# S5 branch of a two-block transformer kernel: chunked states, a table for the tokens inside a chunk, and a new order of steps

## The chip, the cores and the metric

One core of one Trainium2 chip (trn2) runs the whole program. The metric is device microseconds of that core for one execution; smaller is better. Three executions of the kernel before were timed, and one more was taken by the profiler.

## The reference, cut to what matters

Two transformer blocks run one after the other on x of 512 tokens by 1024 channels. The second block has three inputs that meet: an S5 state space branch, a sparse attention branch (called dsa) and two gates. The change touches the S5 branch alone:

```
def s5_branch(xs, a_re, a_im, log_dt, b_re, b_im, c_re, c_im, d_skip, w_glu, b_glu):
    xg = xs.reshape(bsz, seq, 32, 16)          # 32 groups of 16 channels, 64 complex states each
    lb = exp((a_re + i a_im) * dt)             # decay and turn of each state
    bb = (lb - 1) / a * b                      # input matrix
    bu = einsum('blgc,gpc->blgp', xg, bb)
    s[t] = lb * s[t-1] + bu[t]                 # scan over 512 tokens
    y = real(einsum('blgp,gcp->blgc', s, c)) + d_skip * xs
    y = gelu(y)
    val, gate = split(y @ w_glu + b_glu)
    return val * sigmoid(gate)
```

The 2048 complex states are 16 sets of 128 (one set is two groups). Since the decay has a magnitude and an angle, the kernel turns bu back by the angle times t, scans real and imaginary parts with the magnitude alone, and turns the result forward again.

## The kernel before, in words

**Weight stream.** All large matrix products go through 1976 blocks of 128x128 weights, each against 512 tokens. A block is three TensorE instructions (lines 723, 724, 726: high half times high half, low half of the weight, low half of the data). Eight blocks are a unit. A unit is loaded by SP's queue into one of four raw buffers (L2342), rounded to its high half by ScalarE (L1126) into one of four buffers, negated (L1135), and GpSimd's queue adds the rest by an accumulating DMA (L2212). Five units are done by VectorE instead (L2146). Each engine's program walks the same list of blocks with a fixed lead (class Units), so a wait on any one engine ahead of its share of a unit delays all later units.

**First block.** Lines 827 to 861 for TensorE: input products, the recurrent branch, pooling, `w_out`, then 22 pairs of `w_up` tiles (22 times 16 blocks, the loop at L860; called the up stage below) and 8 `w_down` tiles of 22 blocks. ScalarE in this loop does, for each j, the tap of tile j (L1292), the gelu of tile j-1 (L1297), which needs VectorE's two taps of tile j-1 (L1883, L1886), and the tap of tile 22+j. Each is preceded by its share of the weight stream.

**S5 constants.** VectorE makes them in the up and down stages: powers of the angle (L1766), cosines and sines of the first 32 tokens (L1785), then for each of 16 sets a table of cosines and sines of 512 tokens, built by doubling (L1798 to L1816, 18 instructions a set). SP stores each table in memory (`store_table`, L2383) and GpSimd's queue loads it back three sets ahead of use (`load_table`, L2240). The input matrix is formed once (`s5_matrices`, L1915), turned by eight 128x128 transposes on TensorE (`turn_b`, L865), split in high and low halves and spread by 12 DMAs into `wst` (L2436).

**Mixed stage.** After `w_down` and a norm, the first four tiles of `w_in_2` give xs (four tiles of 128 channels). Then five generators on each engine are stepped by one string, ORDER: `d` the attention branch (56 steps), `s` S5 (64), `g` the 16 gate tiles in 64 steps of two blocks, `u` the glu in 32 steps of two blocks, `a` the attention projection in 16 steps of two blocks. The string fixes the order of the instructions on all five engines at once. On TensorE an S5 set takes two matmuls (L925, 96 rows: xs high, low, high against B high, high, low); VectorE turns them (four products, L1987 to L1993), GpSimd adds pairs (L2264, L2266), VectorE scans 512 tokens twice (L1997, L1999) and turns forward (L2002 to L2006); after four sets TensorE sums 16 matmuls of 32 columns over 512 tokens (L914). The high and low halves of xs are stacked in partitions by DMAs from one place of the core's memory to another (L2452; the first two by ScalarE's queue, L1335).

Results in PSUM use eight banks in turn. SBUF slots of 2 KB a partition are given out by `layout`, and a slot's next user waits for the last one.

```
def block(tile, kk, pair, out, start, stop):
    ...
    matmul(out, wh, sr(pair, kk, "hi"), start=start, stop=False)
    matmul(out, wl, sr(pair, kk, "hi"), start=False, stop=False)
    ...
    mm = matmul(out, wh, sr(pair, kk, "lo"), start=False, stop=stop)
```

Of the kernel before, what the change touches and what calls it, by code (L numbers as in the profile page):

```python
# [37 lines left out]
for _n, _c in VECS:  # L38
# [6 lines left out]
         ("lim", 16), ("den", 16), ("ta", 16), ("tb", 16), ("cre", 16), ("cim", 16),   # L45
         ("mod", 48), ("gs1", 8), ("gs2", 8), ("r1", 4), ("r2", 4), ("r", 28), ("wi", 16), ("m8", 8),
         ("need", 1), ("nm", 16), ("rsm", 16)]
# [5 lines left out]
assert _o <= 900  # L53
# [17 lines left out]
UP_STEPS = tuple(int(j > 1 and j % 2 == 0) for j in range(22))  # L71


# [3 lines left out]
def mod_home(u):  # L77
# [6 lines left out]
    "dsssggsdsgdsgsssssggsggsggsdgggsggsssggssggsggsgsgsgssdsssggggssgssgsgsdsgsggdgsgggssgsggg"  # L84
    "ssssggggsgggsdgssssgssgdsssggsgdssggssdgsgdgsdsgdsdudududdudduudugdggduddududuuddduuuuuuud"
    "uududdudgdududdudddduududdddddduaudddduaaaaauaaaaaaaaaa"
)

ROOTS = [1, 2, 3, "ki", "ck", 5, 6]

# [109 lines left out]
class Kit:  # L200


    def __init__(self, nc, top, x_d, w_d, mod_d, cond_d, vec_d, cst_d, inv_d, ssm_d, uk_d, spill_d,
                 tab_d, xs_d, out_d):
# [3 lines left out]
        self.cond_d, self.xs_d = cond_d, xs_d  # L208
# [27 lines left out]
        self.wst_in = sig("wst_in", 16)  # L236
        self.st_in = [sig(f"st_in{i}", 16) for i in range(8)]
        self.tab_out = [sig(f"tab_out{i}", 16) for i in range(2)]
        self.tab_in = [sig(f"tab_in{i}", 16) for i in range(3)]
# [13 lines left out]
        self.sml = sb("sml", [128, 900])  # L253
# [26 lines left out]
    def place_rows(self, part, c):  # L280

        return self.sr("bt", part).rearrange("p (j c n) -> p c j n", c=2, j=4)[:, c]
# [16 lines left out]
def layout(k):  # L299
# [125 lines left out]
    run([("ssm_b",)], 2, top=True)  # L425
    run([("ssm_c",)], 3, top=True)
    run([("uk",)], 2, top=True)
    run([("tabw",)], 4, top=True)

    def constants():  # L430
        for _ in range(8):
            yield
        run([("trig",)], 2)
        take("tq")
        yield
        for _ in range(16):
            yield
        for n in ("tabw", "tq", "trig"):
            give(n)

    consts = constants()
    for _ in range(8):
        next(consts)
# [7 lines left out]
    for j in range(22):  # L451
        take("up", j)
        if j:
            glu_1(j - 1)
        take("up", 22 + j)
        for _ in range(UP_STEPS[j]):
            next(consts, None)
        if j == 11:
            for i in range(NMB):
                give("mb", i)  # L460
            give("cond", 0)
# [5 lines left out]
    for m in range(8):  # L467
        squares("g", m)
        squares(3, m)
        next(consts, None)  # L470
        if m == 4:
            for n in (0, 1):
                take("sq5", n)
            for n in (0, 1):
                give("sq5", n)
        if m == 5:
            for h in ("hi", "lo"):
                run([("bt", h)], 2)
            give("ssm_b")
    for j in range(22):  # L480
        give_pair("act1", j)
    run([("wst", j) for j in range(4)], 8)
    for h in ("hi", "lo"):
        give("bt", h)
# [5 lines left out]
    run([("tbuf",)], 6)  # L490
# [3 lines left out]
    def stacks(s):  # L494
        if s == 0:
            pair("xq", 0)
        for q in (s, s + 1):
            take("st", q)
        if s % 4 == 2:
            give_pair("xq", s // 4)  # L500
            if s < 14:
                pair("xq", s // 4 + 1)

    def s5():
        def outputs(s):
            if s % 4 == 3:
                for q in range(s - 3, s + 1):
                    for n in ("q1", "q2", "q3", "q4"):
                        give(n, q)
                pair("ys", s // 4)  # L510
                give("xs", s // 4)
                give("wst", s // 4)

        stacks(0)
        for s in range(16):
            if s % 2 and s < 15:
                stacks(s + 1)
            give("st", s)
            take("q1", s)
            take("q2", s)  # L520
            yield
            take("q3", s)
            take("q4", s)
            yield
            yield
            if s:
                outputs(s - 1)
                yield
        outputs(15)
        yield  # L530
        give("ssm_c")
        give("tbuf")
        for i in range(7, NMC):
            run([("mc", i)], 2, top=True)
# [157 lines left out]
def tensor_engine(k, T):  # L692
# [166 lines left out]
    done.release(*[("v2", i, h) for i in range(8) for h in ("hi", "lo")])  # L859
    for j in range(22):  # L860
# [4 lines left out]
    def turn_b(c):  # L865

        b = take("s5_turn", c)
        T.wait_ge(at("s5_b"))
        for j in range(4):
            mm = transpose(b[:, 128 * j:128 * j + 128],  # L870
                           k.ssm_b[:, c, 4 * j:4 * j + 4, :].rearrange("p s n -> p (s n)"),
                           k.ident)
        mm.then_inc(*done.tick(("s5_turn", c)))
        give("s5_turn", c)

    for m in range(8):
        tile("w_down", m, range(22), "act1", [3, "g"] if m == 7 else ())
        if m == 5:
            turn_b(0)
            turn_b(1)  # L880
            done.release(("ssm_b",))
# [20 lines left out]
    def s5():  # L902
        def outputs(last):

            j, i = divmod(last, 4)
# [1767 lines left out]
```

## Time and profile before

| what | value |
|---|---|
| median of 3 runs | 1562.13 us (1561.71 to 1562.28) |
| the profiled execution: its span, first to last instruction | 1561.0 us |
| its own time | not given apart from the span; the span lies 1.1 us under the median |
| TensorE matmul busy | 1512.8 us, 97% |
| TensorE weight load busy | 1193.3 us, 76% |
| VectorE busy | 842.4 us, 54% |
| ScalarE busy | 842.2 us, 54% |
| GpSimd busy | 276.5 us, 18% |
| mean granted clock of TensorE | 0.990 |
| moved by DMA | 329.37 MB, 211 GB/s |
| chain that ended last | TensorE 76%, VectorE 14%, ScalarE 5% |

Busy time is a union over one engine's instructions. Matmuls overlap in the pipeline, so the cost of one in a row of its like is the distance from its start to the next start, not its own duration: a block of three costs 0.70 us (three starts 0.23 us apart), while each instruction is shown as about 0.4 us long. A plain fp32 matmul is shown as two records; a transpose is one. The granted clock is a share of full speed, 2.4 GHz; the lower level is 1.2 GHz, shown as 0.5 in a stretch that lies wholly at it.

### The profile page before, as it was taken

How to read it: one execution, taken by the hardware profiler on the slowest of the kernel's cores; microseconds unless marked ns; L12 is line 12 of the kernel's file. 1: busy time of each engine (PE TensorE's matmuls, PEld its weight loads, DVE VectorE, ACT ScalarE, POOL GpSimd, SP SyncE). 2: the span in 40 equal slices, each digit the busy share in tenths (PEclk: the TensorE clock that was granted, in tenths of full speed). 3: DMA queues.
4: the chain of work that ended last, by engine and by line, in shares of the span. 5: the costliest groups of instructions: out<-in, count | busy, mean ns of one | idle time of the engine just before them, and what ended most of it. 6: DMA issues, size and time to landing. Idle time of an engine off the chain costs nothing.

```text
span 1561.0 us, 17900 instructions
## 1 busy us (share of the span) xinstructions
PE 1512.8 (97%) x6688; PEld 1193.3 (76%) x6688; DVE 842.4 (54%) x1640; ACT 842.2 (54%) x1080; POOL 276.5 (18%) x307
## 2 busy tenths in 40 slices
PE   9999999999999999999999897899999999999998
PEld 7877888888878888888877575576777888888886
DVE  6788634555596766545448899975663122110011
ACT  5777877845565555544455353567436444444441
POOL 1111111111111111111114442121011111111111
PEclk9999999999999999999999999999999999999999
DMA  9777787799999988999899894494478998888882
GB/s 266 176 184 170 177 194 184 182 311 299 273 263 265 220 207 210 230 273 241 215 229 291 232 248 130 126 279 167 136 197 201 233 231 182 195 180 194 189 180 81
DMA packets 99221, 329.37 MB, mean 211 GB/s; under 512 B 11568, under 2 KB 13104, under 8 KB 99008
## 3 DMA queue, kind: packets, MB, share of 16 engines
q0 software_dynamic: 36704, 133.56, 45.5%
q1 hardware_dynamic: 58608, 187.33, 35.7%
q10 hardware_dynamic: 3824, 7.34, 1.3%
q8 instruction: 53, 0.87, 0.2%
q14 instruction: 32, 0.26, 0.0%
HBM read 179.69 MB, written 18.87 MB: 127 GB/s over the span
## 4 chain that ended last, share of the span: by engine, by line
PE 76%; DVE 14%; ACT 5%; issue 2%; DMA 2%; POOL 1%; SPq 0%; ACTq 0%; DVEq 0%
PE ps L723 24%; PE ps L726 24%; PE ps L724 24%; DVE pl_f L2052 2%; DVE sml L2049 2%; DVE pl_f L1829 1%; ACT whi L1126 1%; DVE pl_f L1999 1%; DVE pl_r L1546 1%; ACT wlo L1135 1%; POOL pl_f L2264 1%; DMA pl_r<-pl_r 1%; PE ps L767 1%; DMA wlo<-raw 1%; PE ps L914 1%
## 5 line engine op out<-in xcount | busy, mean ns | idle before, releaser
L723 PE MATMUL ps<-pl_r,whi 128*128 128x512 f32 x1976 | 788.9, 399 | 10.0 <-DVE pl_f L1633 3.2
L724 PE MATMUL ps<-pl_r,wlo 128*128 128x512 f32 x1976 | 784.2, 397 | 0.0
L726 PE MATMUL ps<-pl_r,whi 128*128 128x512 f32 x1976 | 784.1, 397 | 0.0
L723 PEld LDWEIGHTS ps<-pl_r,whi 128*128 128x128 f32 x1976 | 373.5, 189 | 108.6 <-issue 13.4
L726 PEld LDWEIGHTS ps<-pl_r,whi 128*128 128x128 f32 x1976 | 373.3, 189 | 91.4 <-DVE pl_r L1563 0.9
L724 PEld LDWEIGHTS ps<-pl_r,wlo 128*128 128x128 f32 x1976 | 373.4, 189 | 89.0 <-issue 0.5
L2212 POOL DMA_DIRECT2D wlo<-raw x238 | 204.0, 859 | 1092.8 <-ACT wlo L1135 1068.2
L1126 ACT ACTIVATE whi<-raw 128x1024 fp32r<-128x1024 f32 x247 | 259.7, 1052 | 185.4 <-PE ps L726 140.1
L1135 ACT ACTIVATE wlo<-raw 128x1024 fp32r<-128x1024 f32 x238 | 248.6, 1045 | 0.0
L1546 DVE TENSOR_TENSOR pl_r<-pl_f,pl_r 128x512 fp32r<-128x512 f32 x120 | 84.5, 704 | 49.3 <-ACT pl_r L1155 32.9
L2184 DVE TENSOR_TENSOR pl_f<-ps,pl_f 128x512 f32<-128x512 f32 x22 | 15.2, 691 | 177.6 <-PE ps L726 177.6
L1292 ACT ACTIVATE pl_f<-ps,vec 128x512 f32<-128x512 f32 x44 | 34.0, 777 | 101.1 <-PE ps L726 101.1
L1155 ACT ACTIVATE pl_r<-pl_f 128x512 fp32r<-128x512 f32 x42 | 26.3, 631 | 106.4 <-DVE pl_f L2184 79.9
L2161 DVE SCALAR_TENSOR_TENSOR pl_f<-ps,sml,pl_f 128x512 f32<-128x512 f32 x16 | 12.0, 750 | 119.8 <-PE ps L726 119.8
L1145 ACT ACTIVATE pl_f<-pl_f 128x512 f32<-128x512 f32 x38 | 23.8, 629 | 73.5 <-DVE pl_f L2161 51.1
L1883 DVE SCALAR_TENSOR_TENSOR pl_f<-ps,vec,pl_f 128x511 f32<-128x511 f32 x44 | 32.9, 748 | 54.1 <-ACT pl_f L1292 54.1
L1829 DVE CUSTOM_DVE_ANT_0 pl_f<-pl_f,pl_f 128x1024 f32<-128x1024 f32 x48 | 58.0, 1219 | 0.1
L1935 DVE TENSOR_TENSOR pl_f<-pl_f,ps 128x512 f32<-128x512 f32 x8 | 5.5, 689 | 62.7 <-PE ps L726 62.7
L1499 ACT ACTIVATE pl_f<-ps 128x512 f32<-128x512 f32 x22 | 13.1, 597 | 45.1 <-PE ps L726 44.9
L1886 DVE SCALAR_TENSOR_TENSOR pl_f<-ps,vec,pl_f 128x511 f32<-128x511 f32 x44 | 33.0, 750 | 1.6
L1646 DVE SCALAR_TENSOR_TENSOR pl_f<-pl_f,pl_f 128x512 f32<-128x512 f32 x20 | 12.9, 689 | 36.2 <-ACT pl_f L1232 36.2
L1633 DVE SCALAR_TENSOR_TENSOR pl_f<-ps,vec,pl_f 128x511 f32<-128x511 f32 (+1 forms) x30 | 22.4, 748 | 17.8 <-ACT pl_f L1213 17.0
(234 smaller groups left out, 1188.3 us busy)
## 6 DMA issues: line engine op xcount, KB each, us to landing
raw<-in_w SPq DMA_DIRECT2D x245, 512.0 KB, 5.3
wlo<-raw POOLq DMA_DIRECT2D x238, 512.0 KB, 6.2
pl_f<-in_mod SPq DMA_DIRECT2D x48, 512.0 KB, 7.3
tab<-pl_f SPq DMA_DIRECT2D x16, 512.0 KB, 6.3
pl_f<-tab POOLq DMA_DIRECT2D x16, 512.0 KB, 7.5
xs<-pl_f SPq DMA_DIRECT2D x16, 256.0 KB, 8.8
pl_f<-xs SPq DMA_DIRECT2D x16, 256.0 KB, 5.1
spill<-pl_f ACTq DMA_DIRECT2D x16, 256.0 KB, 4.8
```

What stands on the lines that cost most here:

```text
L723: matmul(out, wh, sr(pair, kk, "hi"), start=start, stop=False)
L724: matmul(out, wl, sr(pair, kk, "hi"), start=False, stop=False)
L726: mm = matmul(out, wh, sr(pair, kk, "lo"), start=False, stop=stop)
L1126: act(k.whi[:, u % NHI, :], k.raw[:, u % NRAW, :], ACT.Copy).then_inc(*k.w_hi.tick(("w_hi", u)))
L1135: act(k.wlo[:, u % NLO, :], k.raw[:, u % NRAW, :], ACT.Copy, scale=-1.0).then_inc(*k.w_neg.tick(("w_neg", u)))
L1292: act(sb("up", j), ps("w_up", j), ACT.Identity, bias=vc("conv_f_b", j), scale=vc("conv_f_w", 44 + j)).then_inc(*done.tick(("up_tap", j)))
L1546: tt(sr(pair, m, "lo"), src, sr(pair, m, "hi").bitcast(F32), ALU.subtract).then_inc(*done.tick((pair, m, "lo"), *freed_by))
L1829: V.eng.tensor_tensor_reduce(r, r, sb(*c), 1.0, 0.0, ALU.mult, ALU.add, sm("mod", u)).then_inc(*done.tick(("mod_used", u), *([mod_home(u)] ...
L1883: stt(f[:, 1:S], b[:, 0:S - 1], vc("conv_f_w", j), f[:, 1:S], ALU.mult, ALU.add).then_inc(*done.tick())
L1886: stt(f[:, 0:S - 1], b[:, 1:S], vc("conv_f_w", 88 + j), f[:, 0:S - 1], ALU.mult, ALU.add).then_inc(*done.tick(("up", j), ("w_up", j)))
L2049: V.eng.max(m8, cur).then_inc(*done.tick())
L2212: P.eng.dma_start(k.wlo[:, u % NLO, :].bitcast(F32), k.raw[:, u % NRAW, :], accum_op=ALU.add).then_inc(*k.w_lo[u % NLO].tick(("w_lo", u)))
```

## The change

The 16 sets become four groups q of four sets i. A chunk is four tokens (TAPS = 4), so there are 128 chunks (NCH).

- ScalarE writes xs(q) with the four tokens of a chunk apart; SP stores it in memory (`stack_out`) and loads it back (`stack`) with 32 channels times 4 tokens on the partitions and, for each set, 128 chunks along them. This replaces the rounding of xs into halves and the DMAs that stacked them.
- Input: B times the powers 3, 2, 1, 0 of lb (`inputs`, VectorE, 6 instructions of 512 elements a group), turned by 8 transposes a group (`turn_b`), 32 in all instead of 8. For a group TensorE then does 8 plain fp32 matmuls of 128 tokens (chunks) instead of 8 of 512.
- VectorE turns, scans and turns forward 4 sets at once: 4 + 4 products of 512 elements and 8 scans of 128 a group.
- Output: C times the powers 0 to 4 (`outputs`, 6 instructions of 640), and `taps` on TensorE, 32 small matmuls a group: the table of what a token in a chunk adds to itself and to the later ones. The output sums 16 matmuls of 128 from that table and 32 of 127 from the states, all of 32 columns.
- `turning`: cosines and sines of 128 chunks, 14 VectorE instructions a group, instead of 16 tables of 512.
- Constants are made at fixed tiles of the up and down stages (CONSTS for VectorE, TURNS for TensorE and ScalarE), stored by SP one tile later (`stores`), and loaded back as four tables a group, 1.75 MB (`load_tables`), on SP's queue instead of GpSimd's.
- ORDER has 16 steps of S5 instead of 64, done in the order of PLACES, and the other letters stand in a new order among each other.

```
+TAPS = 4
+PLACES = [("b", 0), ("t", 0), ("b", 1), ("c", 0), ("b", 2), ("t", 1), ("c", 1), ("o", 0),
+          ("t", 2), ("b", 3), ("c", 2), ("t", 3), ("c", 3), ("o", 1), ("o", 2), ("o", 3)]
+CONSTS = {2: ("p", 0), 4: ("b", 0), 6: ("c", 0), 8: ("t", 0), 10: ("b", 1), 12: ("c", 1), 14: ("t", 1),
+          16: ("b", 2), 18: ("c", 2), 20: ("t", 2), 22: ("b", 3), 23: ("c", 3), 24: ("t", 3)}
+TURNS = {6: ("b", 0), 8: ("c", 0), 12: ("b", 1), 14: ("c", 1), 18: ("b", 2), 20: ("c", 2),
+         23: ("b", 3), 26: ("c", 3)}
+ORDER = (
+    "dsggsssggggdsggsgsdgssgggddgggsssdsggggdgsgdgsgggsgdggggsgdguuugggduugddggddddgggggddgdgud"
+    "ddugdgggggggdggggddggdgududduuggdudugdudduduuuduuuuudduudududdudduudduddddugaddddduaaauaaaaa"
+    "aaaaaaa"
+)
 # TensorE, up and down stages
+    def taps(q):
+        T.wait_ge(at("s5_c", q), at("s5_b", q))
+        for i in range(4):
+            for c in range(2):
+                for r in range(TAPS):
+                    mm = matmul(b[rows, 128 * i + 32 * r:128 * i + 128]...,
+                        sb("sbp")[:, 512 * c + 128 * i + 3:512 * c + 128 * i + 128:TAPS],
+                        cp[:, c, 0:TAPS - r, i], start=c == 0, stop=c == 1,
+                        tile_position=(0, 32 * r))
     for j in range(22):
         tile("w_up", j, range(8), "h2")
         tile("w_up", 22 + j, range(8), "h2")
+        turns(j)
 # TensorE, S5
-        for s in range(16):
-                matmul(b, k.wst[0:96, j, i, c, :], sr("st", s)[0:96], start=True, stop=True)
+            if step == "b":
+                for c in range(2):
+                    T.wait_ge(at("bt", q), at("st", q))
+                    for i in range(4):
+                        mm = matmul(b[:, cols], sb("bt", q)[...], sb("st", q)[:, cols], ...)
+            elif step == "o":
+                for n in range(TAPS):
+                    for i in range(4):
+                        matmul(y[32 * i:32 * i + 32, NCH * n:NCH * n + NCH], sb("tt", q)[...],
+                               sb("st", q)[:, 128 * i:128 * i + 128], ..., tile_position=(0, 32 * i))
+                for c, state in ((0, "q1"), (1, "q3")):
+                    for n in range(TAPS):
+                        for i in range(4):
+                            mm = matmul(y[32 * i:32 * i + 32, NCH * n + 1:NCH * n + NCH], ...,
+                                sb(state, q)[:, 128 * i:128 * i + 127], ...)
 # VectorE, constants
+    def outputs(q):
+        V.wait_ge(done.now(), at("ssm"), at("bt_out", q), *freed("scp"))
+        if q:
+            V.wait_ge(at("s5_taps", q - 1), at("cp_out", q - 1))
+        tt(re, cre, lr, ALU.mult).then_inc(*done.tick())
...
 # SP
     for j in range(22):
         if j > 1:
             weights(16)
+        if j:
+            stores(j - 1)
...
+    load_tables(0, "bt", "cs", "tt", "cp")
     weights(32)
+    def stack_out(q):
+        Q.wait_ge(at("xs", q))
+        dma(k.stk_d[q], sb("xs", q)).then_inc(*k.st_out[q].tick(("xs_out", q)))
+    def stack(q):
+        Q.wait_ge(at("xs_out", q), *freed("st", q))
+        dma(sb("st", q).rearrange("p (i n) -> p i n", i=4),
+            k.stk_d[q].rearrange("(i c) (j n) -> (c j) i n", i=4, j=TAPS)).then_inc(
+            *k.st_in[q].tick(("st", q)))
+    for q in range(4):
+        stack_out(q)
+    stack(0)
+    load_tables(1, "bt", "cs", "tt", "cp")
     def s5():
+        for step, q in PLACES:
+            if step == "b" and q < 3:
+                stack(q + 1)
+            if step == "t" and q in (0, 1):
+                load_tables(q + 2, "bt", "cs", "tt", "cp")
+            yield
```

All four tables of a group share one semaphore, so each is counted as there when the last of the four has landed. `outputs(q)` uses the buffer from which the turned B of the same group is stored (`bt_out`), for its products in between.

## Rows read from the trace of the kernel before

**Rows 1.** The page's part 2: busy tenths in 40 slices of 39 us

```profile
PE   9999999999999999999999897899999999999998
DVE  6788634555596766545448899975663122110011
PEclk9999999999999999999999999999999999999999
DMA  9777787799999988999899894494478998888882
```

**Rows 2.** Windows: up stage and mixed stage; stretch length, busy by engine, clock, DMA

```profile
405.00:750.00 345.00, 344.84 (x1491) 278.07 (x1490) 220.67 (x525) 179.08 (x215) 52.20 (x62) 1.00 0.94 238
819.26:1100.32 281.06, 253.55 (x1229) 181.53 (x1227) 228.87 (x439) 152.38 (x249) 87.44 (x83) 0.96 0.74 207
```

**Rows 3.** Waits of TensorE between 815 and 1115 us: total us, times, longest

```profile
PE ps L809 <- DVE sml L1541: 6.2, 1, 6.2
PE ps L965 <- DVE pl_f L2130: 5.3, 1, 5.3
PE ps L914 <- DVE pl_f L2006: 4.4, 1, 4.4
PE ps L925 <- DMA pl_r<-pl_r: 3.5, 1, 3.5
...
PE ps L981 <- DVE pl_f L2060: 1.5, 1, 1.5
PE ps L987 <- ACT pl_f L1368: 1.4, 1, 1.4
PE ps L925 <- DVE pl_f L1975: 1.1, 1, 1.1
```

**Rows 4.** Timeline of TensorE: start us, us of the merged run, line, count

```profile
931.48 0.63 PE L925 MATMUL ps<-pl_r,pl_r 96*128 96x512 f32 x2
932.04 3.64 PE L914 MATMUL ps<-pl_f,pl_f 128*32 128x512 f32 x32
935.61 0.50 PE L723 MATMUL ps<-pl_r,whi 128*128 128x512 f32 x1
...
1094.82 2.38 PE L1020 MATMUL ps<-cst,pl_f 128*128 128x128 f32 x20
1097.14 1.09 PE L1031 MATMUL ps<-cst,sml 128*64 128x128 f32 x16
1098.07 2.32 PE L1040 MATMUL ps<-pl_f,pl_f 128*64 128x512 f32 x16
```

**Rows 5.** Groups of VectorE between 815 and 1115 us, forms apart

```profile
L1997 DVE TENSOR_TENSOR_SCAN pl_f<-ps,pl_f 128x512 f32<-128x512 f32 x16 | 19.6, 1223 | 2.9 <-POOL pl_f L2264 2.8
...
L1987 DVE TENSOR_TENSOR pl_f<-ps,pl_f 128x512 f32<-128x512 f32 x16 | 10.9, 683 | 9.0 <-PE ps L925 9.0
...
L2074 DVE TENSOR_TENSOR_SCAN pl_f<-pl_f 128x384 f32<-128x384 f32 x1 | 1.0, 960 | 0.0
...
L2074 DVE TENSOR_TENSOR_SCAN pl_f<-pl_f 128x256 f32<-128x256 f32 x1 | 0.7, 692 | 0.0
```

**Rows 6.** The page's part 6: DMA issues, KB each, median us to landing

```profile
wlo<-raw POOLq DMA_DIRECT2D x238, 512.0 KB, 6.2
...
tab<-pl_f SPq DMA_DIRECT2D x16, 512.0 KB, 6.3
...
xs<-pl_f SPq DMA_DIRECT2D x16, 256.0 KB, 8.8
pl_f<-xs SPq DMA_DIRECT2D x16, 256.0 KB, 5.1
```

**Rows 7.** Timeline of ScalarE and GpSimd around the end of one `w_up` tile

```profile
573.03 0.78 ACT L1292 ACTIVATE pl_f<-ps,vec 128x512 f32<-128x512 f32 x1 [2.41 <-PE ps L726]
573.71 1.05 ACT L1126 ACTIVATE whi<-raw 128x1024 fp32r<-128x1024 f32 x1
...
576.00 0.85 POOL L2212 DMA_DIRECT2D wlo<-raw  x1 [4.23 <-ACT wlo L1135]
```

More of the change, by code:

```diff
@@ L424, in layout @@
         give("x", m)
[L425 to L443, printed above, removed]
+    for n, w in (("ssm_b", 2), ("ssm_c", 2), ("trig", 2), ("sbp", 2), ("sbt", 2), ("scs", 2),
+                 ("scp", 3), ("stt", 1)):
+        run([(n,)], w, top=True)
     def glu_1(j):
@@ L469, in layout @@
         squares(3, m)
[L470 to L479, printed above, removed]
     for j in range(22):
         give_pair("act1", j)
-    run([("wst", j) for j in range(4)], 8)
-    for h in ("hi", "lo"):
-        give("bt", h)
+    for n in ("ssm_b", "ssm_c", "trig", "sbp", "sbt", "scs", "scp", "stt"):
+        give(n)
+    run([("uk",)], 2)
+    for q in range(4):
+        for n in TABS:
+            run([(n, q)], TABS[n][1] // S)
     give("sq", "g", 0)
@@ L489, in layout @@
         take("xs", j)
-    run([("tbuf",)], 6)
+    for q in range(4):
+        take("st", q)
     for m in range(8):
         give("xw", m)
[L494 to L502, printed above, removed]
-    def s5():
[L505 to L514, printed above, removed]
-        for s in range(16):
[L516 to L520, printed above, removed]
-            yield
[L522 to L532, printed above, removed]
+    def s5():
+        for step, q in PLACES:
+            if step == "t":
+                for n in ("q1", "q2", "q3", "q4"):
+                    take(n, q)
+            elif step == "c":
+                give("bt", q)
+            elif step == "o":
+                for n in ("q2", "q4", "q1", "q3"):
+                    give(n, q)
+                for n in ("cs", "tt", "cp"):
+                    give(n, q)
+                give("st", q)
+                take("yg", q)
+                give("xs", q)
+                pair("ys", q)
+                give("yg", q)
+            yield
         for i in range(7, NMC):
@@ L919, in s5 @@
-        take("mags")
-        for s in range(16):
-            j, i = divmod(s, 4)
-            for c in range(2):
-                b = take("bu", c, s)
-                T.wait_ge(at("wst"), at("st", s))
-                matmul(b, k.wst[0:96, j, i, c, :], sr("st", s)[0:96], start=True, stop=True).then_inc(
-                    *done.tick(("bu", c, s), *([("st", s)] if c else []),
-                               *([("wst", j)] if c and i == 3 else [])))
-                give("bu", c, s)
-            yield
-            yield
-            yield
-            if s:
-                outputs(s - 1)
-                yield
@@ L1303, in scalar_engine @@
         up(22 + j)
+        turns(j)
     gelu(21)
@@ L1819, in vector_engine, with s5_constants @@
+    def s5_constants(n):
+        what, q = CONSTS.get(n, (None, 0))
+        if what == "p":
+            powers()
+        elif what == "b":
+            inputs(q)
+        elif what == "c":
+            outputs(q)
+        elif what == "t":
+            turning(q)
     steps = 0
@@ L2423, in sync_engine @@
         dma(sb("xw", m), k.xs_d[m]).then_inc(*k.x_in[m].tick(("x_back", m)))
-    Q.wait_ge(*freed("ssm_b"), *freed("ssm_c"))
-    dma(k.ssm_b, k.ssm_d[:, 0:2]).then_inc(*k.ssm_in.tick())
-    dma(k.ssm_c[:, 0:2], k.ssm_d[:, 2:4]).then_inc(*k.ssm_in.tick(("ssm",)))
+    for m in range(8):
+        weights(8)
+        stores(21 + m)
+        weights(14)
+    for u in units.ahead():
+        load(u + NRAW)
+    load_tables(0, "bt", "cs", "tt", "cp")
     Q.wait_ge(*freed("uk"))
     dma(k.uk, k.uk_d).then_inc(*k.uk_in.tick(("uk",)))
-    for m in range(8):
-        weights(22)
-        if m:
-            store_table(8 + m)
```

546 lines of the change are left out of this document (295 added, 251 removed).

## The prediction

> **What bounds the kernel now.** First the page's slices: TensorE is at 9 tenths nearly everywhere, so work taken from another engine pays only where TensorE waits for it; VectorE is full in slices 21 to 25, and there TensorE dips [rows 1]. Then two windows. In the up stage TensorE is busy 344.84 of 345 us at clock 1.00: nothing can be gained there, and each microsecond of new TensorE work costs one. In the mixed stage (281.06 us from the first S5 matmul to the end of attention) it is busy 253.55 us, so 27.5 us are idle, at a mean clock of 0.96 [rows 2]. A clock of 0.96 with 0.5 as its lower level means 8% of the stretch, 22.5 us, at half speed, in which 11 us were lost. The waste is some 38.7 us. Its waits [rows 3]: 6.2 for a reciprocal on VectorE, 5.3 and 4.4 and 1.5 and 1.1 for VectorE (a reciprocal is nothing in itself: VectorE is late, with 228.87 busy us in 281), 1.4 for ScalarE, 3.5 for the stacking DMA. These sum to 23.4; some 4 us are small waits of attention, on rows not shown, which the change does not touch.
>
> **VectorE gets light in the mixed stage.** Before: 16 sets by eight products of 0.683 us and two scans of 1.223 us [rows 5], 87.4 + 39.1 = 126.5 us. After: 4 groups by eight products, 21.9 us, and 32 scans of 128 elements. The scans of 384 and 256 take 0.960 and 0.692 [rows 5], so 128 less is 0.27 less, and one takes 0.43: 13.7 us. Gone are 91 us of 229, and 138 in a stage of 240 to 280 us no longer set the pace. S5 is then done after about 27 g steps; attention gets its VectorE time when it asks. I take the VectorE waits and ScalarE's as gone (19.9 us); what is late next is the entry.
>
> **The entry of the mixed stage.** S5's first group needs xs through memory. It is written after xs(3) at about 808 us; a store of xs takes 8.8 us to land, a load back 5.1 [rows 6]. The sum is 822 us; the new load has pieces of 512 bytes, no row shows such a one, and between no more than 5.1 and twice that I add 1.5. The order asks for it at 819.3, after step d: a wait of 4 us (0 to 12). The second group's turned B shares a semaphore with 1.75 MB of tables issued right behind that load, some 9 us at the stage's 207 GB/s [rows 2], so they land at about 826 if nothing else is under way, and TensorE asks at 826, two g (2.8 us) after its first; weights and stacks share the engines: 3 us more (0 to 8). After a wait of 3.5 to 6 us the trace shows a stretch at the lower clock: 3.5 us lost. The traffic of this entry (three groups of tables, 5.5 MB, stacks and saves, beside the weights) meets DMA engines that are 8 to 9 tenths busy already in slices 21 to 23 [rows 1]: 3 us for late weights (0 to 10). With attention's 4 us, new waste is 4 + 3 + 3.5 + 3 + 4 = 17.5 us against 38.7: **21.2 us gained**, between 33 (only attention's waits and 2 more stay) and 1.
>
> **TensorE work, outputs.** One group of 16 matmuls of 32 columns by 512 took 935.61 - 932.04 = 3.57 us [rows 4], four of them 14.3 us. After: 48 matmuls by 128 a group, 192 in all, 384 records. If four neighbours overlap as before, the tokens streamed are 12 times 128 a group against 4 times 512: 3/4 of 14.3, 10.7 us. If each record costs what the nearest shape does (64 columns by 128: 16 records in 98.07 - 97.14 = 0.93 us, 0.058 each [rows 4]), it is 22.3 us. That row is at two neighbours at once and is full with 128 tokens, so it excludes no more than it shows; I take 12, nearer the same-width row: **-2.3**. The input matmuls: two of 512 took 932.04 - 931.48 = 0.56 us here [rows 4] and 0.47 where a block follows, 7.5 in all; 32 plain ones of 128 are 64 records of 0.11 (a transpose is 2.32/20 = 0.116 with its lead-in [rows 4]), 7.0: **-0.5**.
>
> **TensorE work, constants.** 24 more transposes at 0.116: **+2.8**. Taps, 128 matmuls, 256 records: overlapped in fours, the widest of each four sets 32 times 128 tokens, two records of 0.112 (3.57/8 for 512 tokens, a quarter of it for 128): 7.1 us; at 0.058 a record 14.8; with no overlap (80 tokens on average) 18. I take 7.5, for the output row shows the overlap: **+7.5**. All of it lies in the up and down stages where TensorE is full, so all of it shows.
>
> Here the Trainium skill speaks against the change. TensorEngine Tiling (Array Packing), section Instruction Overhead, says each matmul has about 60 cycles of overhead on trn2 and warns against taking the tiling factor from a dimension that is already small. Sixty cycles at 2.4 GHz are 25 ns a record, an estimate from that page, and 640 records at 25 ns are 16 us against my 19.5: by it the sum would stay. Tensor Engine: Matmul & The Clock Gate, section Back-to-back issue gap, gives about 81 ns for each load and matmul pair of 128 tokens, and by it outputs and taps would take 52 us. Row L1031 at 58 ns already contradicts the 81; no row here is shorter than its streaming, so no run shows the 25.
>
> **VectorE, ScalarE and SP in the up stage.** VectorE's constants: 12 products of 512 and 640 a group and 14 short ones, some 14.4 us a group, 58 us, and 5 us of powers, against 16 tables of about 4.9 us and the old matrix: less than before, with VectorE at 221 of 345 us [rows 2]. Covered by TensorE's lead in eight banks. But `outputs(q)` waits for the store of the turned B. Relative to the end of the w_up pair in which the turn stands: transposes 0.9, ScalarE's two copies to 2.4, its next unit to 4.4, accumulate landed 6.2 later (the tile of the row: tap at 573.03, accumulate issued at 576.00 [rows 7], [rows 6]), and only then does SP, which waits for that unit, come to the store: about 11, landed at 17 (14 to 21). Six products of 0.83 end it at 22, two taps at 23.6. TensorE asks for its taps at 23.3 and ScalarE's gelu, which then waits 5 us, holds the conversion that TensorE needs at about 36 and gets at 33. So this stall of VectorE for 15 us, four times, is just covered: **+1** (0 to 24). If the cover goes, TensorE stops for weights, since gelu stands ahead of them on ScalarE.
>
> GpSimd loses 16 table issues and 24 of 32 additions, SP gains 16 table loads, 32 stores and 8 stack transfers for 16 stores and 60 small ones: at 0.3 to 0.6 us of issue they hide behind its waits for units. The powers and the smaller stack rounding cost nothing on the path.
>
> **Sum.** -21.2 - 2.3 - 0.5 + 2.8 + 7.5 + 1 = -12.7 us. From the span of 1561.0 that is 1548.3; the median of the runs lies 1.1 us above it, so 1549.4, told as **1549**. A measurement of this kernel can tell about 0.2%, 3.1 us, from no change.
>
> **Rivals.**
> 1. *The entry is smooth too.* The store lands sooner than its median and the tables with it: only 6 us of waste stay, 11.5 less than above: 1538. For it: the old stacks made their first date. Chance 0.18.
> 2. *The entry becomes the new wait.* Stack and tables queue behind each other on SP; 12 us at the first group, 8 at the second, 10 for weights, 5 lost at the lower clock, 4 for attention, 39 in all: what was won on VectorE is lost at DMA, and the 8.5 us of the other terms stay: 1571. For it: DMA full in these slices [rows 1], one semaphore for four tables. Against: 5.5 MB are fewer than the tables of before. Chance 0.13.
> 3. *Slower in the up stage.* The store of the turned B lands past 17 us; VectorE's stall outlasts ScalarE's and TensorE's lead, four times 5 us idle plus 1.5 at the lower clock: 26 - 1 more, 1574. It decides at 18 us from pair end to landing. Against: 3 us of slack by the sum above. Chance 0.09.
> 4. *Small matmuls have a floor.* 0.058 us for each of 640 records: 37.1 instead of 19.5, 17.6 more: 1567, slower. It decides from (19.5 + 12.7)/640 = 0.050 us a record. For it: no row has a shorter record with 128 tokens. Against: 32 output records in 3.57 us keep four at once. Chance 0.14. The Trainium skill's page TensorEngine Tiling (Array Packing) has such an overhead, but at 25 ns, with which this rival falls.
>
> **How the numbers follow.** The forecast has 0.46, and its bounds (entry and weights some 9 either way, small matmuls -2 to +6) reach from 1540 to 1560. Faster: 0.44 of it and all of rival 1, 0.62. Within 0.2% (1559 to 1565.3): 0.02 of it and 0.06 of rivals 2 and 4, 0.08. Slower: the rest, 0.30. The range that leaves out no more than 0.2 takes half of rival 1 and of rival 3 in: 1537 to 1573.
>
> **What would show it.** Right: up stage longer by 10 to 13 us, still over 99% busy; L914's successors in 2.7 to 3.2 us a group; VectorE near 140 us in the mixed stage, with no wait of TensorE for it over 2 us; one or two DMA waits at the first S5 matmuls. Wrong: clock under 1.00 in the up stage with waits on `wlo` (rival 3), taps over 3 us a group (rival 4), or more than 15 us of DMA waits at the entry (rival 2).

## The result and the profile after

The changed kernel takes 1527.12 us (median of 4 runs, 1525.85 to 1528.67) against 1562.2 us of the kernel before beside it: ratio 0.9766, 95% interval 0.9743 to 0.979. The forecast was 1549, the range 1537 to 1573: faster was right, the size was not. The profiled execution took 1528.67 us, its span is 1527.4.

The page's slices, as in [rows 1] (PE, VectorE, clock, DMA):

```profile
PE   9999999999999999999997999999999999999998
DVE  5788643555596958443134457925663212110011
PEclk9999999999999999999998999999999999999999
DMA  9777887799999798799879867986587998888882
```

Counted from one (the prediction counts the slices from zero), VectorE is full in one slice of the mixed stage only, the 26th, where before it was full or nearly so in five. TensorE dips once, in slice 22, the entry of the mixed stage. The same two windows as [rows 2], the second from the first S5 matmul to the last of attention (columns: PE, weight load, VectorE, ScalarE, GpSimd, clock, DMA share, GB/s):

```profile
405.00:750.00 345.00, 343.63 (x1740) 281.40 (x1739) 206.11 (x380) 185.24 (x232) 51.42 (x60) 1.00 0.91 232
821.00:1070.80 249.80, 238.16 (x1515) 183.78 (x1515) 140.52 (x340) 154.73 (x247) 61.49 (x54) 0.98 0.78 219
```

The mixed stage is 31 us shorter, and VectorE has 140.52 busy us in it instead of 228.87. Waits of TensorE between 815 and 1115 us, as [rows 3]:

```profile
PE ps L900 <- DMA pl_f<-stk: 8.7, 1, 8.7
PE ps L1011 <- ACT pl_f L1404: 1.5, 1, 1.5
PE ps L900 <- DMA pl_f<-tab: 1.5, 1, 1.5
```

None for VectorE is left in this view. The new one is the second group's stack; the 1.5 us for tables come later, at the input step of the fourth group (871.79). Timeline of TensorE at the entry (start, duration, line, count, then the wait ahead of it):

```profile
821.01 1.95 PE L900 MATMUL ps<-pl_f,pl_f 128*128 128x128 f32 x16
822.71 0.48 PE L687 MATMUL ps<-pl_r,whi 128*128 128x512 f32 x1
...
834.43 3.75 PE L900 MATMUL ps<-pl_f,pl_f 128*128 128x128 f32 x16 [8.71 <-DMA pl_f<-stk]
837.83 0.77 PE L687 MATMUL ps<-pl_r,whi 128*128 128x512 f32 x1
```

And of SP's queue:

```profile
814.57 0.38 SPq L2514 DMA_DIRECT2D pl_f<-stk  x1
814.99 3.06 SPq L2451 DMA_DIRECT2D pl_f<-tab  x4
818.15 1.19 SPq L2375 DMA_DIRECT2D raw<-in_w  x2
819.39 0.42 SPq L2514 DMA_DIRECT2D pl_f<-stk  x1
```

The first group (821.01) does not wait at all. The second stack is issued at 819.39, behind four tables and two units of weights, and takes 14.9 us to land. After the 8.7 us the sixteen matmuls take 3.75 us instead of 1.95: the clock is at its lower level (the mean from 825 to 850 us is 0.80). Without this stack TensorE would still have waited from 825.7 to 828.0, when the last table of group 1 landed.

Three pieces of new TensorE work: eight transposes, one group's taps, one group's outputs (L910 and L919).

```profile
479.22 1.03 PE L831 MATMUL ps<-cst,pl_f 128*128 128x128 f32 x8
...
502.76 1.93 PE L845 MATMUL ps<-pl_f,pl_f 128*32 128x128 f32 x64 [0.53 <-DVE pl_f L1863]
...
857.87 1.08 PE L910 MATMUL ps<-pl_f,pl_f 128*32 128x128 f32 x32
858.76 1.92 PE L919 MATMUL ps<-pl_f,pl_f 128*32 128x127 f32 x64
```

Over the whole run, none of these is off its forecast price by more than about 1 us. What it had not priced is in a stretch that the change doesn't touch. The window from 1200 to 1500 us holds little but blocks of weights in both kernels. Before:

```profile
1200.00:1500.00 300.00, 300.00 (x1288) 241.71 (x1287) 44.32 (x68) 133.65 (x157) 45.65 (x53) 1.00 0.86 202
```

After:

```profile
1200.00:1500.00 300.00, 300.00 (x1312) 246.15 (x1312) 42.68 (x65) 131.32 (x152) 46.85 (x55) 1.00 0.85 196
```

TensorE is never idle and its granted clock is 1.00 in both, yet it does 1312 matmuls instead of 1288. From start to start a block matmul takes 0.2289 us after and 0.2333 before, in every stage. There are 5928 of them, and 4.4 ns each is 26 us. The weight buffers and the blocks are the same. What moved is the SBUF: the change adds 161 columns of small constants (`SMALL`), and behind them the pool of 2 KB slots begins at byte 73408 of a partition instead of 72768. The block matmuls read their data from these slots, and their weights from buffers that did not move.

### The profile page after: what moved, and what is told of

The parts are those of the page before. It is cut to its first block, busy times and chain, and to the rows that moved or that the text cites. A ratio compares the mean times of both kernels' runs of the same rounds, so it can differ in the third digit from the quotient of the medians.

```text
span 1527.4 us, 18719 instructions
## 1 busy us (share of the span) xinstructions
PE 1492.1 (98%) x7256; PEld 1207.9 (79%) x7256; DVE 732.5 (48%) x1373; ACT 854.1 (56%) x1099; POOL 248.8 (16%) x275
## 4 chain that ended last, share of the span: by engine, by line
PE 80%; DMA 8%; DVE 6%; ACT 4%; issue 1%; SPq 1%; POOL 0%; ACTq 0%; DVEq 0%
PE ps L687 25%; PE ps L688 25%; PE ps L690 24%; DMA wlo<-raw 3%; DMA raw<-in_w 2%; DVE pl_f L1914 1%; DMA pl_f<-stk 1%; ACT whi L1117 1%; ACT wlo L1126 1%; DMA tab<-pl_f 1%; PE ps L731 1%; DVE pl_r L1527 1%; PE ps L1011 1%; PE ps L1031 1%; DMA pl_f<-tab 1%
## 5 line engine op out<-in xcount | busy, mean ns | idle before, releaser
L688 PE MATMUL ps<-pl_r,wlo 128*128 128x512 f32 x1976 | 775.3, 392 | 0.0
L687 PEld LDWEIGHTS ps<-pl_r,whi 128*128 128x128 f32 x1976 | 372.5, 189 | 101.9 <-issue 15.2
L1527 DVE TENSOR_TENSOR pl_r<-pl_f,pl_r 128x512 fp32r<-128x512 f32 x116 | 80.3, 692 | 44.7 <-ACT pl_r L1146 28.3
L2231 DVE TENSOR_TENSOR pl_f<-ps,pl_f 128x512 f32<-128x512 f32 x22 | 15.2, 691 | 172.9 <-PE ps L690 172.9
L1968 DVE SCALAR_TENSOR_TENSOR pl_f<-ps,vec,pl_f 128x511 f32<-128x511 f32 x44 | 32.8, 745 | 14.7 <-ACT pl_f L1283 14.7
L1855 DVE TENSOR_TENSOR pl_f<-pl_f,sml 128x640 f32<-128x640 f32 x4 | 3.3, 824 | 57.8 <-DMA tab<-pl_f 57.8
```

Source lines behind the costliest of these rows:

```text
L1527: tt(sr(pair, m, "lo"), src, sr(pair, m, "hi").bitcast(F32), ALU.subtract).then_inc(*done.tick((pair, m, "lo"), *freed_by))
L1968: stt(f[:, 1:S], b[:, 0:S - 1], vc("conv_f_w", j), f[:, 1:S], ALU.mult, ALU.add).then_inc(*done.tick())
```

## The experiments

Lengths by stage come from the profiled executions: from the start to the first S5 matmul, from there to the last attention matmul (the mixed stage), and the rest. "Pace" is the mean distance from one block matmul to the next. Kernels run beside each other share a measurement of the kernel before; it came out between 1562.2 and 1566.9 us, so ratios and lengths of stages compare better than times.

### Is the pace the place of the slots?

The first edit, in one kernel or the other:

```
-        self.base = (nc.sbuf_base + 31) // 32 * 32
+        self.base = (nc.sbuf_base + 31) // 32 * 32 + 640    # or 64, 128, 192, 256
```

b_base640 gives the kernel before the base of the changed one.

> The kernel before with its pool of 2 KB slots 640 bytes higher, at the address it has in the changed kernel (73408 instead of 72768); no instruction differs. In the changed kernel a matmul of a block starts every 0.2296 us instead of every 0.2333 (96 of them in 22.1 us), in every stage. Theory A, where the slots lie sets the pace of the block matmuls: 5928 times 0.0036 us, 21 us faster, 1541 us. Theory B, the pace comes with the changed program and not with the address: no change, 1562 us, pace 0.2333.

> The kernel before, slots 128 bytes higher (72896). Theory A, if only the place within 256 bytes counts (both 72896 and 73408 leave 192, 72768 leaves 64): 1541 us, pace 0.2296. If it is the distance to something else, or a larger period: 1562 us. Theory B: 1562 us.

> The kernel before, slots 256 bytes higher (73024, which leaves 64 of 256 like 72768). Theory A with a period of 256 bytes: no change, 1562 us, pace 0.2333. Theory A as a matter of distance or of a longer period: some other pace. Theory B: 1562 us.

> The changed kernel, slots 128 bytes higher (73536, which leaves 64 of 256, as the kernel before has it). Theory A with a period of 256 bytes: 21 us slower, 1548 us, pace 0.2333. Theory A with another period: in between or no change. Theory B: no change, 1527 us.

| kernel | slots moved by, bytes | pace, us | first S5 at | mixed stage | rest | time |
|---|---|---|---|---|---|---|
| before | 0 | 0.2333 | 819.3 | 280.8 | 460.9 | 1562.1 |
| b_base256 | 256 | 0.2333 | 821.6 | 281.4 | 460.9 | 1565.4 (one run) |
| b_base128 | 128 | 0.2289 | 810.3 | 280.5 | 456.6 | 1548.9 (one run) |
| b_base640 | 640 | 0.2289, in part 0.2333 | 816.1 | 280.8 | 456.4 | 1550.0 |
| after | 640 | 0.2289 | 821.0 | 249.8 | 456.6 | 1527.1 |
| a_base128 | 768 | 0.2333 | 831.7 | 249.4 | 461.0 | 1543.4 (one run) |

b_base640 was 0.9894 of before (0.9869 to 0.992), 16.5 us less than the 1565.5 us beside it. Theory A had said 21, and 5928 times 4.4 ns are 26; so the pace moved as it said and the time by less (why is taken up below). The changed kernel at the slow place has the count of the kernel before, and the kernel before at the fast place that of the changed one. a_base128:

```profile
1200.00:1500.00 300.00, 300.00 (x1287) 241.74 (x1286) 42.95 (x66) 131.17 (x153) 46.47 (x54) 1.00 0.85 196
```

b_base128:

```profile
1200.00:1500.00 300.00, 300.00 (x1312) 246.14 (x1311) 43.43 (x66) 134.14 (x157) 47.36 (x55) 1.00 0.88 205
```

So the pace goes with the place, not with the program. Is it the slots' own address, or their distance from the weight buffers? b_all128 moves both by 128 bytes, b_w128 moves the weights by 128 and the slots by 256:

```
+        self.shift = sb("shift", [128, 32])
         self.raw = sb("raw", [128, NRAW, UB * 128])
```

> The kernel before with a tensor of 128 bytes a partition put ahead of everything, so that the weight buffers and the slots both lie 128 bytes higher. Theory A1 (the absolute address of the slots decides, 192 modulo 256 fast, 64 slow): a block matmul starts every 0.229 us, time 1547 to 1551. Theory A2 (the distance between the slots and the weight buffers decides): it stays at 0.2333 us, time 1561 to 1566.

> The kernel before with its weight buffers 128 bytes higher and its slots 256 bytes higher: the slots' own address is what it was, modulo 256 (64), their distance from the weight buffers is 128 more. Theory D (the distance decides): a block matmul every 0.229 us, time 1547 to 1553. Theory A1 (the slots' own address, which b_all128 already spoke against) or chance by the run: 0.2333 us, time 1561 to 1567, or runs of both kinds.

b_all128: 0.2333 us, 1566.14 us in one run. b_w128: 0.2289 us, 1548.09 us, 0.9907 of before (0.9871 to 0.9943), where the slots' own address is what it was modulo 256. So it is the distance between the slots and the buffers ahead of them that decides; of these the block matmuls read the weight buffers. Then the steps between:

> The kernel before with its slots 64 bytes higher. Theory D with steps of 128 (slow at 0 and 256, fast at 128): in between, either level, or one of its own between 0.229 and 0.2333 us if the cost is graded. No number is excluded; a time of 1547 to 1566.

> The kernel before with its slots 192 bytes higher. Theory D, if half of each 256 bytes is fast and half slow: the level of b_base64 or the other one, so that of 64, 128 and 192 two neighbours agree. A time of 1547 to 1566.

192 bytes gave 0.2324 us up to 915 us and again from 1008 to 1161, and 0.2333 otherwise, 1563.3 us in one run. 64 bytes gave a third level, 0.2267 us, and the fastest kernel before: 1535.74 us in one run (802.6, 281.2 and 450.3 by stage). b_base64:

```profile
1200.00:1500.00 300.00, 300.00 (x1326) 248.47 (x1325) 43.50 (x66) 134.77 (x157) 47.46 (x55) 1.00 0.87 201
```

The two expectations had offered two levels or something graded; it is graded: 0.2333, 0.2267, 0.2289, 0.2324 to 0.2333, 0.2333 us at 0, 64, 128, 192 and 256 bytes. That had to hold in the changed kernel too, where 640 + 192 is 64 modulo 256:

> The changed kernel with its slots 192 bytes higher, which puts their distance from the weight buffers, modulo 256, where b_base64 had it. Theory D (the distance sets the pace, whatever the program): a block matmul starts every 0.227 us instead of 0.229; over 5928 of them 13 us less, of which the mixed stage may keep some 2 for itself; time 1512 to 1516, 0.967 to 0.970 of before. Chance, or a pace bound to the program: 0.229 us, 1525 to 1529.

The pace was 0.2267 us as theory D said, the time 1519.18 us, 0.9714 (0.9695 to 0.9732): faster than the changed kernel (a_again, below: 0.9759), but by 7 us (0.0045 of 1563) and not by 13. TensorE gets to its waits sooner: it waits 6.9 us for weights instead of 5.6, 9.4 instead of 8.7 for the second group's stack and 1.7 instead of 1.5 for the fourth group's tables. The same holds at the slow end: 5208 matmuls outside the mixed stage by 4.4 ns would be 23 us between a_base128 and the changed kernel, and 15 arrived (18 against a_again). In the mixed stage nothing arrived in either kernel (280.8 against 280.5, 249.4 against 249.8).

The pace isn't wholly fixed by the place. In seven of the twelve traces at the distance of 128 bytes, modulo 256, it was 0.2333 us for a part of the run. b_base640 falls to it after a wait of 1.9 us at 434.8 and is back at 742, a_best (below) falls after one of 2.0 us at 1142.4 and stays. The others (a_stack2, a_stack4, a_dveload, a_oldorder, a_oldorder2) have it for 20 to 50 us each. In four of the seven the fall comes after a wait of 1.9 to 3.3 us with a stretch at the lower clock behind it. Neither is needed: a_stack2 falls at 522.7 us in a row of block matmuls without a gap, and is back at 551 after eight transposes. Its window, where the changed kernel has 112 matmuls:

```profile
524.00:549.00 25.00, 25.00 (x109) 20.26 (x108) 23.00 (x37) 13.62 (x16) 4.05 (x5) 1.00 1.03 268
```

None of the four traces at 0 or 256 bytes was ever fast, and the three at 64 kept 0.2267 in 1200 to 1500. What in the chip makes the distance count, and what makes the pace change at one distance, was not tried.

### Is it VectorE's relief, or the new order?

a_dveload puts VectorE's load back in amount, not in its old places: five products at each g of the string:

```
     for c in ORDER:
         if c in gens:
             next(gens[c], None)
+        for _ in range(5 if c == "g" else 0):
+            V.wait_ge(done.now())
+            tt(sm("pc", 0, 144), sm("ps", 0, 144), sm("ps", 0, 144), ALU.mult).then_inc(*done.tick())
```

> The changed kernel with VectorE's old load put back and nothing else: at each of the 64 g steps VectorE writes five products of 144 columns into constants that nobody reads any more, some 0.30 us each by the row of the 128-column product, 96 us in all against the 91 that the change took away. Theory R (the mixed stage got shorter because VectorE was relieved): VectorE is at 236 busy us again, its waits come back, the stage of 250 us grows by 15 to 25, time 1542 to 1552. Theory O (the new order of steps and fewer S5 steps did it, whatever VectorE's load): the stage grows by under 4, time 1527 to 1531.

a_oldorder takes the new order away:

```
-    "dsggsssggggdsggsgsdgssgggddgggsssdsggggdgsgdgsgggsgdggggsgdguuugggduugddggddddgggggddgdgud"
...
+    "dsggdsssgdgggsggsgsgdssggggggssssgggggsggsgdggsgggggdsgggdgggggggggggggggdgggdgggdggdggdgdd"
...
```

> The changed kernel with the letters d, g, u and a of ORDER in the relative order of the kernel before, and its 16 S5 steps put in at the same counts of g steps as in the changed one. Theory R (relief of VectorE): the stage keeps nearly all its gain, time 1527 to 1533. Theory O (the new order did it): a good part of the 31 us comes back as waits of TensorE in attention and its clock falls, time 1537 to 1555.

| order | VectorE in the mixed stage, us | mixed stage | time, ratio |
|---|---|---|---|
| old, before | 228.9 | 280.8 | |
| old, a_oldorder | 138.2 | 269.6 | 1548.19, 0.9885 (0.9864 to 0.9906) |
| new, a_dveload | 249.3 | 309.1 | 1585.89, 1.0123 (1.0092 to 1.0154) |
| new, after | 140.5 | 249.8 | 1527.12, 0.9766 (0.9743 to 0.979) |

Both expectations were too simple, and each theory held half. The new S5 work in the old order brings 11 us, and the new order 20 more. a_dveload came out far above both of its ranges: the load was 108.8 us, 0.348 each, where 96 were expected, and the stage is 28 us longer than before. Its VectorE is busy 20 us more than before, so these 28 us are not the price of the order alone. Waits of TensorE in a_dveload, 815 to 1115 us:

```profile
PE ps L996 <- DVE sml L2138: 35.5, 1, 35.5
PE ps L900 <- DMA pl_f<-stk: 9.5, 2, 8.1
PE ps L773 <- DVE sml L1522: 4.9, 1, 4.9
```

The new order asks for attention's selection early; a VectorE that is busy can't have it done, and TensorE stands still for 35.5 us. In this wait VectorE works at that selection and, for 20.6 us, at the products put back, so its length is also one of where they were put. In a_oldorder, the same view, then the stage and two windows in it:

```profile
PE ps L898 <- DMA pl_f<-stk: 15.2, 2, 12.9
PE ps L954 <- DVE pl_f L2175: 3.9, 1, 3.9
PE ps L685 <- ACT pl_f L1442: 2.0, 1, 2.0
PE ps L994 <- DVE sml L2136: 1.8, 2, 1.2
```

```profile
823.80:1093.70 269.90, 243.93 (x1518) 188.65 (x1516) 138.20 (x340) 149.52 (x243) 60.72 (x54) 0.96 0.72 203
...
910.00:940.00 30.00, 30.00 (x135) 23.65 (x134) 2.47 (x5) 15.52 (x20) 5.15 (x6) 1.00 0.93 231
...
970.00:1000.00 30.00, 26.13 (x102) 18.29 (x101) 28.24 (x68) 14.64 (x24) 3.90 (x4) 0.94 0.57 141
```

VectorE is light in total and still late: 2.47 busy us of 30 from 910 us, where its next piece waits 26.0 us for results of attention whose matmuls TensorE reaches at 935.9 in this order, and 28.24 of 30 from 970, with TensorE waiting and at clock 0.94. In the changed kernel TensorE is busy all of the time from 880 to 1060 us, at clock 1.00. A further part of the difference is at the stacks. The two waits for them:

```profile
836.33 2.02 PE L898 MATMUL ps<-pl_f,pl_f 128*128 128x128 f32 x16 [2.32 <-DMA pl_f<-stk]
857.24 3.11 PE L898 MATMUL ps<-pl_f,pl_f 128*128 128x128 f32 x13 [12.92 <-DMA pl_f<-stk]
```

The long one is at the third group; the next expectation overlooked this and took both for the second.

> As a_oldorder (the letters d, g, u and a in the relative order of before), with the second stack issued right behind the first. In a_oldorder TensorE waits 15.2 us for stacks against 8.7 in the changed kernel. Theory S (the old order costs mostly through where it puts the second group's input step): the stage of 269.6 us falls to 258 or less, time 1534 to 1539. Theory O (the new order is worth its 20 us through attention and the filling of VectorE's time): it falls by 3 to 6 only, time 1542 to 1546.

The stage was 270.7 us, the time 1549.88 (0.9913, 0.989 to 0.9935), a smaller fall than either theory gave, none in fact. The second group's 2.3 us are gone, and the third group waits 14.7 us instead of 12.9: its stack, not issued ahead, stands behind eight saves of attention and a group of tables. So this run could not decide between the theories, and the old order with all four stacks issued ahead was not run. Timeline of SP:

```profile
831.72 7.23 SPq L2536 DMA_DIRECT2D xs<-pl_f  x8
838.99 3.94 SPq L2449 DMA_DIRECT2D pl_f<-tab  x4
843.03 0.39 SPq L2512 DMA_DIRECT2D pl_f<-stk  x1
```

So the order string sets SP's queue as well as VectorE's. By the two traces, TensorE is idle 26.0 us of the stage in a_oldorder and 11.6 in the changed kernel. Of these 14 us, 5 are waits for stacks and tables (15.2 against 10.2) and the other 9 are waits of other kinds, mostly in attention; the mean clock of 0.96 against 0.98 makes the rest, about 6 us.

### The entry

In a_stack2 the second stack goes ahead of the tables:

```
     stack(0)
+    stack(1)
     load_tables(1, "bt", "cs", "tt", "cp")
...
-            if step == "b" and q < 3:
+            if step == "b" and 0 < q < 3:
```

> The changed kernel with the load of the second group's stack issued right behind the first, ahead of the four tables of group 1. Theory E (the wait of TensorE for the second stack, 8.7 us in the trace, is one of a queue: the load stands behind 1.75 MB of tables and two units of weights, and the low clock after it, some 4 us, comes from it): both go, time 1514 to 1519. Rival: the transfers themselves fill the window (DMA at its full share from 822 to 838 us), so the wait moves to a unit of weights or the tables, time 1523 to 1528.

1521.63 us, 0.9719 (0.9695 to 0.9742), between the two ranges; the mixed stage is 244.6 us. Half of theory E: 8.7 us became 4.5, and the stretch at the lower clock 3.4 us long instead of 10.2. The next wait stands behind it. The view names no releaser:

```profile
PE ps L900 <- issue: 4.5, 1, 4.5
```

The landings do. The second stack was there at 822.3, and the last table of group 1, issued at 819.61, took 11.8 us and landed at 831.42; TensorE goes on at 831.51. The timelines of SP and TensorE:

```profile
817.95 2.05 SPq L2451 DMA_DIRECT2D pl_f<-tab  x4
...
831.51 2.90 PE L900 MATMUL ps<-pl_f,pl_f 128*128 128x128 f32 x12 [4.47 <-issue]
```

a_best also moved the second group's input step (`"dsggsggggssdsggs..."` in place of `"dsggsssggggdsggs..."`), a_again is the changed kernel beside it.

> The changed kernel as it is, beside the next two on the same chip, so that they have a common measure. Every theory: 0.974 to 0.979 of the kernel before.

> The changed kernel with the second stack issued right behind the first (as in a_stack2) and, in ORDER, the second group's input step four g steps (eight blocks, 5.5 us) later. Theory Q (what is left of the entry wait, 4.5 us in a_stack2, is the time that the loads of stack and tables still need when TensorE gets there): the wait goes to zero and the stage is 4 to 5 us shorter than in a_stack2, 8 to 10 shorter than in the changed kernel, time 1516 to 1519 where the changed kernel has 1527. Rival: the later input step makes the first attention or gate tiles, or the first states, late, and the wait comes back there: within 2 us of a_stack2.

a_again: 1525.28 us, 0.9759 (0.9737 to 0.9781). a_best: 1528.29 us, 0.9782 (0.9753 to 0.9811), no gain. The second group (833.79) no longer waits, but the step also sends the third stack, which now stands behind group 2's tables:

```profile
833.79 2.02 PE L900 MATMUL ps<-pl_f,pl_f 128*128 128x128 f32 x16
851.09 3.75 PE L900 MATMUL ps<-pl_f,pl_f 128*128 128x128 f32 x16 [9.77 <-DMA pl_f<-stk]
```

So the wait came back, as the rival said, but at the third stack and larger than either had it: the mixed stage is 249.3 us, 4.7 longer than in a_stack2 and as long as in the changed kernel. In the profiled execution, the longest of the four at 1535.65 us, the slower pace from 1142 us on costs 8 us more. The last step was to issue all four stacks at the start, two ahead of the tables and two behind:

> The changed kernel with all four stacks issued at the start: the first two ahead of the four tables of group 1, the last two right behind them, none any more inside the S5 steps. Theory Q (place in the queue): no stack is waited for after the second, which keeps some 4 us; the stage is 243 to 246 us long, time 0.970 to 0.973 of before. Rival (the DMA engines are full from 815 to 850 us, so what is loaded sooner makes something else late): the third and fourth stack delay the units of weights, waits of the same size at those, the stage 248 to 252.

The mixed stage is 243.8 us, the time 1523.49 (0.9748, 0.9716 to 0.978). No stack after the second is waited for, as theory Q said; the 4.4 us of the second group stay, and again end with its last table (831.04, TensorE goes on at 831.13). The ratio lies above the expected 0.970 to 0.973 and cannot tell it from a_again; the stage, 5 us shorter, can. Its rest is 456.9 us against 453.1, for its clock is at the lower level for 10.2 us from 1135.

### TensorE's constants

In `taps`, the four sets are done twice (32 matmuls more a group, 64 records; the expectation's "64 more" are the records):

```
-        for i in range(4):
+        for i in (0, 1, 2, 3, 0, 1, 2, 3):
```

> The changed kernel with each group's 32 small matmuls of the table issued twice, results unchanged (64 more per group in program, 7.5 us more on TensorE by 1.86 us a group in the trace, four groups). Theory C (constants in the up stage cost TensorE's time one for one, nothing hides them): time 1534 to 1535.5. Rival: some of it falls into waits that are there anyway, time 1528 to 1532.

1532.61 us, 0.9785 (0.9762 to 0.9808). A group now takes

```profile
502.73 3.68 PE L845 MATMUL ps<-pl_f,pl_f 128*32 128x128 f32 x128 [1.85 <-DVE pl_f L1863]
```

instead of 1.93. Its first S5 matmul is at 828.6 us, a_again's at 822.0: 6.6 us for 7.4 of work, and the wait for `wlo` in the up stage went from 1.4 to 0.6. Up to there, constants on TensorE cost one for one but for the waits that they fill. The whole time says less: it lies between the two ranges, and by the ratios it is 3 to 4 us above the changed kernel's (0.9766 and 0.9759), with an interval as wide as that.

### Together

a_final has the distance of a_base192 and the stacks of a_stack4.

> The same distance, and all four stacks issued at the start as in a_stack4. If the two add: 13 us and 3 to 4 us less than the changed kernel, time 1508 to 1513, 0.964 to 0.968 of before. If a faster pace only makes TensorE reach the second stack sooner and wait for it: as a_base192.

1514.81 us (1513.83 to 1515.47), 0.9686 (0.9672 to 0.97), and a_base192 beside it 1519.18. They add: 4.4 us for the stacks, the mixed stage 243.6 against 249.4. It is above the expected 1508 to 1513, for this counted 13 us for the pace, which alone had given 7. It is the fastest kernel of the study, 12 us under the changed one.

## Why the prediction was wrong, and where it was right

The change's own effect is read at the same pace, the kernel before against a_base128: spans 1561.0 and 1542.1, -18.9 us where the sum had -12.7. The two were not measured beside each other, and a_base128 is one run: against the 1565.5 us beside it, it is -22. At the old place the time, 1543.4, would have lain in the range. The place of the slots gives the rest, -14.7 by the spans (1542.1 to 1527.4); by a_again's span, 1524.1, it is -18.0, for that execution has no stretch at the lower clock around 1140 us where the other has one (0.81 from 1125 to 1150).

- **The step that failed: no term for the blocks.** The prediction took what it did not see edited as unchanged: 1976 blocks stood in no term, and 3 x 1976 matmuls at 4.4 ns less were, at 26 us by count and 15 to 18 as measured, worth more than its whole sum. With the forecast's own terms and this one, 1549.4 - 14.7 = 1534.7, outside its range. The other 6 us or so are terms of its own that were too small, waste in the mixed stage above all. No row of the kernel before could price it, for all its blocks run at one level; but the diff showed that buffers moved, and the range held nothing for it.
- **VectorE.** Right: 138 us forecast, 140.52; a scan 0.398 us for 0.43; all waits for it gone. The reason given was half: "attention gets its VectorE time when it asks" needs the new order, for which the prediction has no term. In the old order the same S5 work brings 11 us.
- **Waste in the mixed stage: 17.5 us forecast.** In a_base128 TensorE is idle 10.0 of 249.4 us, and at clock 0.99 some 2.5 are lost: 12.6. So 26.1 us were gained, not 21.2. Terms: first group 4, measured 0 (in the changed kernel the load had landed at 819.8 us and TensorE came at 821.0); second group 3, measured 7.7 (its stack); the fourth group's tables, in no term, 0.9; attention 4, measured 1.5; lower clock 3.5, measured 2.5; late weights 3, none in this stage.
- **Outputs.** -2.3 forecast, -3.3 measured: 2.74 us a group, 0.0286 a record, against 12/4 = 3.0. **Input** 1.70 a group, 6.8 for 7.0. **Transposes** 0.79 for eight, so 24 are 2.4 for 2.8. **Taps** 1.86 to 1.89 a group, 7.5 for 7.5. Good to 0.4 us each, outputs to 1.
- **The stage before S5** grew by 12.4 us at the same pace; forecast 11.3 (2.8, 7.5 and 1). The stall of VectorE is there, 57.8 us in four on its store, and is covered: TensorE waited 0.7 us for taps in all. Which part holds the last us wasn't tried.
- **Rival 4** (a floor of 0.058 us a record) falls: 0.0286. The row that it came from had two neighbours at once and the new work has four. The Trainium skill, TensorEngine Tiling (Array Packing), section Instruction Overhead, has 60 cycles, an estimate of 25 ns: the trace agrees that a record costs no less. **Rival 3** falls: the up stage keeps clock 1.00 with TensorE busy 343.63 of 345. **Rival 2** was right in its place, the stack in SP's queue, and too dear: 8.7 us at the second group, 1.5 for the fourth group's tables and none at the first. **Rival 1** was right for the first group alone.

## What to carry to other kernels

A sum over the edits holds only if the rest keeps its speed: compare the commonest instruction's pace in both traces first, and where an edit resizes anything in SBUF, run the kernel before at the new addresses too. When an engine is relieved, cost the order of the steps for every queue that the order drives; here the same string was worth 20 us on a light VectorE, and on one loaded beyond its old measure the stage was 28 us longer than before. A DMA that a step issues inherits what that step put ahead of it: twice (a_best, a_oldorder2) a stack issued ahead left the next one waited for, and with all four issued at the start only the tables were. Before explaining a wait, look which group it is at and what landed last before it ended.

## What the runs showed of the hardware

The pace of an fp32r matmul of 128x128 by 512 goes with the distance in SBUF between the weights and the data that it reads, modulo 256 bytes: 0.2333 us at 0 (as the kernel before has it) and at 256, 0.2267 at 64, 0.2289 at 128, 0.2324 to 0.2333 at 192, at granted clock 1.00 in the windows counted. This holds in both kernels at 0, 64 and 128; 192 and 256 were run in the kernel before alone. For the kernel before the best place made 1536 us (one run) of the 1563 beside it. At 128 bytes the pace changed to 0.2333 in seven of twelve traces, for about 20 us up to the rest of the run, four times after a wait of TensorE and a stretch at the lower clock, and once with no gap at all. It came back in six, in four of them at the eight transposes. Four neighbouring matmuls of 32 columns by 128 tokens overlap to 0.029 us a record.
